# V rows of a PEER layer summed on TensorE as two column tiles of 64, with new places for the work of the next block

## The reference, cut to what matters

```python
def peer_ffn(h, w_q, keys, u, v):
    ...
    experts = ...                      # (token, 8 heads, 16): 128 expert numbers a token, of 16384
    g = jax.nn.softmax(best_s, axis=-1)
    def block(args):                   # 128 tokens at a time
        xt, et, gt = args
        act = jax.nn.gelu(jnp.einsum('td,thkd->thk', xt, u[et]), approximate=False)
        return jnp.einsum('thk,thkd->td', gt * act, v[et])
```

## Time and profile before

| | before |
|---|---|
| device time, median of 3 | 3504.54 us |
| device time of the profiled execution | 3502.22 us |
| its span, first to last instruction | 3500.1 us |
| granted TensorE clock, mean | 0.940 |
| bytes moved by DMA | 1346.12 MB, mean 385 GB/s |

### The profile page before, as it was taken

The page is one execution under the profiler, slowest core; times in us unless marked ns, Lnnn a source line. Parts: engine busy times, 40 slices in busy tenths (PEclk is TensorE's granted clock), DMA queues, the critical chain, the costliest instruction groups (busy, mean ns, idle before and its releaser), DMA issues.

```text
span 3500.1 us, 34723 instructions
## 1 busy us (share of the span) xinstructions
PE 2942.9 (84%) x10960; PEld 1660.0 (47%) x10960; DVE 2341.0 (67%) x5884; ACT 814.6 (23%) x1924; POOL 2008.2 (57%) x2085
## 2 busy tenths in 40 slices
PE   7786898888997899888987799888998789976777
PEld 6465355533554355444554445544554445522222
DVE  6229756886578765887477855786648866596554
ACT  3111421133111422133211332114221232211111
POOL 1003765666565664666555655666547655577775
PEclk9897999999999999999999999999999999998999
DMA  7787999999999999999999999999999999999998
GB/s 275 259 299 266 409 409 409 408 409 402 409 402 408 399 405 403 407 409 390 405 409 408 397 351 409 409 408 370 354 409 409 409 346 350 390 404 410 409 409 339
DMA packets 387256, 1346.12 MB, mean 385 GB/s; under 512 B 41793, under 2 KB 44865, under 8 KB 386433
## 3 DMA queue, kind: packets, MB, share of 16 engines
q0 software_dynamic: 294912, 1073.87, 78.0%
q1 hardware_dynamic: 91008, 265.83, 20.1%
q10 hardware_dynamic: 1152, 4.19, 0.3%
HBM read 1334.03 MB, written 35.39 MB: 391 GB/s over the span
## 4 chain that ended last, share of the span: by engine, by line
PE 43%; DMA 25%; DVE 14%; POOL 9%; issue 6%; ACT 3%; SPq 0%; DVEq 0%; ACTq 0%; POOLq 0%
PE ps_sum L1212 19%; DMA rows<-in_peer_u,ids_u 9%; PE ps_p L979 7%; DMA rows<-in_peer_v,ids_v 6%; DMA rows<-in_peer_v,ids_u 5%; POOL rows L802 5%; PE ps_s L1127 5%; POOL rows L792 4%; DVE rows L1986 4%; DMA w_ring<-packed 2%; PE ps_s L1065 2%; PE ps_p L1073 2%; DVE feat_b L1873 1%; PE ps_p L1047 1%; DVE feat_b L1869 1%
## 5 line engine op out<-in xcount | busy, mean ns | idle before, releaser
L1212 PE MATMUL ps_sum<-rows,diag 128*128 128x512 f32 x3584 | 1748.0, 631 | 271.9 <-DMA rows<-in_peer_v,ids_v 129.2
L1986 DVE CUSTOM_DVE_ANT_0 rows<-h_cur,rows 128x1024 f32<-128x1024 f32 x1024 | 1228.1, 1220 | 539.7 <-DMA rows<-in_peer_u,ids_u 527.0
L792 POOL DMA_INDIRECT rows<-in_peer_u,ids_u x1024 | 1005.4, 982 | 720.7 <-issue 498.8
L1212 PEld LDWEIGHTS ps_sum<-rows,diag 128*128 128x128 f32 x3584 | 684.1, 201 | 1166.4 <-issue 1047.8
L802 POOL DMA_INDIRECT rows<-in_peer_v,ids_v x512 | 493.5, 964 | 452.2 <-PE ps_sum L1212 295.6
L802 POOL DMA_INDIRECT rows<-in_peer_v,ids_u x512 | 494.4, 966 | 267.8 <-issue 127.3
L1466 ACT ACTIVATE diag<-ident,acts 128x128 f32<-128x128 f32 x896 | 327.4, 394 | 1057.4 <-PE ps_sum L1212 757.5
L979 PE MATMUL ps_p<-hT,w_ring 128*128 128x128 f32 x2944 | 367.8, 286 | 36.1 <-DMA w_ring<-packed 18.0
L979 PEld LDWEIGHTS ps_p<-hT,w_ring 128*128 128x128 f32 x2944 | 362.0, 202 | 68.6 <-issue 42.3
L1772 DVE CUSTOM_DVE_ANT_0 e<-ps_s,bias_t 128x256 f32<-128x256 f32 (+6 forms) x96 | 74.2, 773 | 177.5 <-PE ps_s L1065 70.6
L2007 DVE SCALAR_TENSOR_TENSOR x_cur<-rows,acts,x_cur 128x1024 f32<-128x1024 f32 x128 | 164.0, 1282 | 13.4 <-DMA rows<-in_peer_v,ids_v 13.4
(11 more groups left out here) (280 smaller groups left out, 2325.7 us busy)
## 6 DMA issues: line engine op xcount, KB each, us to landing
w_ring<-packed SPq DMA_DIRECT2D x343, 512.0 KB, 7.7
w_ring<-in_wstream SPq DMA_DIRECT2D x65, 512.0 KB, 5.3
packed<-in_wstream SPq DMA_DIRECT2D x49, 512.0 KB, 7.9
rows<-in_peer_u,ids_u POOLq DMA_INDIRECT x1024, 13.3
rows<-in_peer_v,ids_u POOLq DMA_INDIRECT x512, 10.7
rows<-in_peer_v,ids_v POOLq DMA_INDIRECT x512, 15.4
bias_rows<-rows SPq DMA_DIRECT2D x5, 1024.0 KB, 12.8
bias_t<-in_x SPq DMA_DIRECT2D x8, 512.0 KB, 6.2
```

The source lines that it names most:

```text
L792: pool.indirect_dma_start(u_rows[:, j % G_RING, :], None, peer_u, bass.IndirectOffsetOnAxis(ap=ids_u[:, j:j + 1], axis=0)).then_inc(u_land ...
L1212: ins = pe.matmul(ps_sum[:, c * 512:(c + 1) * 512], diag[:, n % 4, :], v_rows[:, j % G_RING, c * 512:(c + 1) * 512], start=(n == 0), stop= ...
L1986: dve.tensor_tensor_reduce(row, h_cur[:, :], row, 1.0, 0.0, ALU.mult, ALU.add, dots[:, p:p + 1]).then_inc(u_used, 1)
```

## The change

- V rows are summed in pairs. A gather of V no longer brings one row to each of 128 tokens, but two rows to each of 64: in an even gather partitions 0 to 63 and 64 to 127 hold two experts each of tokens 0 to 63, in an odd gather those of tokens 64 to 127. The diagonal matrix becomes 128x64, a 64x64 diagonal in its upper and in its lower half (`ident_pair` scaled by `coef`), so a product sums both halves. The even row goes to output partitions 0 to 63 (`low`), the odd row to 64 to 127 (`high`): two column tiles of TensorE. `add_rows` works on a pair at every odd position, with products in the order low, high, low, high, and waits for both rows' gathers and diagonals.
- All 128 rows go to TensorE; the eighth that VectorE took (`on_vector`, L2007, `v_added`) is gone.
- Expert numbers, gates and GELU results have to stand in the new order of partitions: `by_group` makes four copies of a quarter each where one stood (`hand_first_ids`, `hand_gates`, `hand_last_ids` on VectorE, the GELU on ScalarE). All V gathers now take `ids_v`.
- There are 8 diagonal buffers of 64 columns in place of 4 of 128. Some constants share memory with `acts` or `cols`.
- All three tables of stops have new numbers, other ones for each body.

The core of the diff; of the tables, which are long, the first body of TensorE's and VectorE's is shown in part:

```diff
 TENSOR_STOPS = [
...
-     "mla_2": (32, 33, 35), "mla_3": (35, 35, 37), "diff_0": (37, 38, 40, 41), "diff_1": (41, 43, 43, 44),
-     "diff_2": (45, 47, 48, 49), "diff_3": (49, 49, 51, 51), "join": (54, 56), "mix_out": (56, 56, 58, 58, 58),
-     "norm_cross": (59, 62), "cross_q": (62, 62, 62, 67, 67), "cross_scores": (69,), "cross_mix": (70, 73, 74),
...
+     "mla_2": (34, 34, 35), "mla_3": (35, 35, 35), "diff_0": (35, 43, 43, 43), "diff_1": (43, 43, 43, 50),
+     "diff_2": (50, 50, 50, 50), "diff_3": (50, 50, 55, 55), "join": (62, 62), "mix_out": (62, 62, 62, 62, 62),
+     "norm_cross": (62, 62), "cross_q": (62, 62, 62, 67, 67), "cross_scores": (67,), "cross_mix": (67, 73, 73),
...
 VECTOR_STOPS = [
...
-     "choose_0": (104, 105, 105, 105, 106, 108, 108, 108, 108, 111, 111), "top_1": (113, 113, 113, 113, 114, 117),
-     "choose_1": (120, 120, 124, 125, 126, 126, 126, 128, 128, 128, 128)},
...
+     "choose_0": (108, 108, 108, 108, 111, 111, 111, 111, 111, 111, 111), "top_1": (122, 122, 122, 122, 122, 122),
+     "choose_1": (122, 122, 122, 122, 122, 122, 122, 122, 122, 122, 122)},
...
-        diag = sb("diag", [P, 4, P])
+        diag = sb("diag", [P, DIAGS, GROUP])
+        ident_pair = sb("ident_pair", [P, GROUP])
...
+        def by_group(first, last):
+            for at, own in ((low, low), (low, high), (high, low), (high, high)):
+                column = slice(first + (own is high), last, 2)
+                row = slice(first + (at is high), last, 2)
+                yield at, column, own, row
...
-            def add_row(bp, p):
-                bp, j = row_of(bp, p, SUM_LAG)
-                if j is not None and not on_vector(j):
-                    n = sum_index(j)
-                    pe.wait_ge(diag_made, bp * SUM_ROWS + n + 1)
+            def add_rows(bp, p):
+                bp, last = row_of(bp, p, SUM_LAG)
+                if last is None or last % 2 == 0:
+                    return
+                pair = (last - 1, last)
+                pe.wait_ge(diag_made, bp * EXPERTS + last + 1)
+                for j in pair:
                     pe.wait_ge(v_landed[j % G_RING], bp * (16 * EXPERTS // G_RING) + 16 * (j // G_RING + 1))
...
-                    for c in range(2):
-                        ins = pe.matmul(ps_sum[:, c * 512:(c + 1) * 512], diag[:, n % 4, :], v_rows[:, j % G_RING, c * 512:(c + 1) * 512],
-                                        start=(n == 0), stop=(n == SUM_ROWS - 1), skip_group_check=True)
-                    ins.then_inc(v_used, 1)
+                for c in range(2):
+                    for j, own in zip(pair, (low, high)):
+                        ins = pe.matmul(ps_sum[own, c * 512:(c + 1) * 512], diag[:, j % DIAGS, :], v_rows[:, j % G_RING, c * 512:(c + 1) * 512],
+                                        start=(last == 1), stop=(last == EXPERTS - 1), skip_group_check=True)
+                        if c:
+                            ins.then_inc(v_used, 1)
...
-                    act.activation(acts[:, s * STEP:(s + 1) * STEP], dots[:, s * STEP:(s + 1) * STEP], ACT.Gelu).then_inc(acts_made, 1)
+                    for at, column, own, row in by_group(s * STEP, (s + 1) * STEP):
+                        ins = act.activation(acts[at, column], dots[own, row], ACT.Gelu)
+                    ins.then_inc(acts_made, 1)
...
-                    act.wait_ge(v_used, bp * SUM_ROWS + (n + SUM_SLOTS - 3))
-                    act.activation(diag[:, n % 4, :], ident[:, :], ACT.Copy, scale=coef[:, j:j + 1]).then_inc(diag_made, 1)
+                    act.wait_ge(v_used, bp * EXPERTS + (j + G_RING - DIAGS + 1))
+                    act.activation(diag[:, j % DIAGS, :], ident_pair[:, :], ACT.Copy, scale=coef[:, j:j + 1]).then_inc(diag_made, 1)
...
-                if j is not None and on_vector(j):
...
-                    dve.scalar_tensor_tensor(x_cur[:, :], v_rows[:, j % G_RING, :], coef[:, j:j + 1], x_cur[:, :], ALU.mult, ALU.add)\
-                       .then_inc(v_added, 1)
```

263 lines of the change are left out of this document (138 added, 125 removed), and 52 rows, old and new, of tables (SCALAR_STOPS, VECTOR_STOPS).

## The result

The changed kernel is slower: 3610.51 us at the median of five runs (3603.0 to 3631.6), beside 3504.54 us for the kernel before. The ratio is 1.0318, with a 95% interval of 1.0284 to 1.0351. The forecast was 3434 us.

The account below looks back on a forecast made before the run. Bound: DMA transfers at 409 GB/s, with TensorE limiting the dips. 3502.2 - 79 (dips) + 2 + 5 + 5 (what stays) + 1.5 (start) - 5.5 (end) = 3431.2; with 2.3 to the median, 3434 us; range 3415 to 3500.

Parts of the forecast that it names:

- The ceiling: From 350 us on, DMA transfers set the pace wherever the rate is 409 GB/s; a faster engine gives nothing there.
- TensorE is the limit there: In three short dips of the transfer rate (14.9, 19.6, 23.7 us), TensorE, 90 to 93% busy, sets the pace.
- rival 4: Dips stay because something other than TensorE, an attention chain, makes them: 3500 to 3505 us; chance 0.08 together with rival 3.
- The factor of 0.571: TensorE's V sums: both tiles of a pair overlap, so a block takes 111 us in place of 195.
- TensorE's busy time with 0.43 of L1212 taken away, against what the DMA needs: In the dips: 55.6, 68.5, 73.0 us against 65.1, 80.4, 76.3, so the DMA becomes the limit; 2 us stay.
- The turns: TensorE drains at tiling mode changes: 0.2 us each, two per group of pairs, 7 us a body against 84 saved.
- one position later: V ring: a pair's even buffer comes free only with the odd one, 2.56 us later; no cost was summed.
- rival 3: The ring of 8 V buffers becomes the bound and GpSimd stands there: about 3500 us; chance 0.08 together with rival 4.
- The stops: New stops make longer front end bursts; the DMA runs dry 4 us in the first body, 5 us in all.
- rival 2: Tiles overlap in part, or new stops leave gaps (28 us): either about 3460 us, both 3490; chance 0.12.
- The end: After the last gather, TensorE's V sums keep up with the DMA and finish 5.5 us earlier.
- rival 1: TensorE's two column tiles run one after the other: 3575 us, between 3540 and 3640; chance 0.14.

Follow-up runs that it names:

- the kernels with 64 and 72 columns: Kernel before with only the first of each V row's two products, made 64 or 72 columns wide in place of 128: 3525.0 us and 3495.1 us.

## Why the prediction was wrong

The ladder, in ratios to the kernel before times 3504.5 us; each step carries 6 to 16 us of uncertainty:

| step | from, to | us |
|---|---|---|
| TensorE's V work halved | 1, 0.9965 | -12 |
| its products 64 columns wide: turns | 0.9965, 1.0059 | +33 |
| the rest of the tiles: second products, VectorE's rows, copies, GELUs | 1.0059, 1.0087 | +10 |
| both rows of a pair waited for together | 1.0087, 1.0171 | +29 |
| the new stops | 1.0171, 1.0318 | +52 |

The steps join different kernels, and each says what its edit did in that place. The +33 of the turns was measured on a kernel with 298 of them each way and half of the products; the changed kernel has 158, and what they cost there was not measured.

**The ceiling** held: no slice of the changed kernel is above 409 GB/s, and it moves the same 1346 MB. It is not the same on every chip (361 GB/s on one of the slower ones).

**"TensorE is the limit there"** held in part. Its V products, which stand between the links of the attention, could be halved for 12 us; its value products, which are links themselves, counted for 20 to 31 of 34 us. So it is TensorE's work in the order of the chain that the dips wait for, more than its total load. Of rival 4, a chain of the attention, the part that names something other than TensorE has no support in ScalarE's link; the value products were halved on the slower chips only, and VectorE's links were not tried.

**The factor of 0.571** held: a pair costs 1.72 us, 1.74 were taken. L1210's busy time is 1225 us and not 900 to 1100; a part of it ran at half the clock (3.68 us a pair).

**The step that failed first** is "TensorE's busy time with 0.43 of L1212 taken away, against what the DMA needs". It subtracted work at a clock of 0.96 and kept that clock for the rest. The halved products show what comes in its place: 62 us of work away in the dips, 12 us of time gained, TensorE still 86 to 88% busy, at 0.76 to 0.85. That the lower clock takes most of the difference is read from the traces: the rest of TensorE's work in the attention of bodies 3 to 6 grew from 147 to 183 us of busy time while L1212's fell from 158 to 109, and two executions of the same instructions differ by 8 us in one body at clocks of 0.74 and 0.84. By the estimate above some 30 us of the dips hang on the clock. The 16 to 20 us that would stay at full clock are a second error of the same step: it let the transfers run at 409 GB/s as soon as TensorE's busy time was below theirs, although the heads' chain leaves TensorE idle between links (43 of 348 us in these stretches before, 64 of 356 with half of the products). No run changes the clock and nothing else, and the one that raised it did so by work of its own. The prediction named this for the last block's retrieval ("the clock can take some of it back"), found it covered there by the transfers, and didn't ask it of the dips, where the transfers don't cover it.

**The turns** were priced and then not summed. The estimate of 0.2 us a drain was right in size (0.20 and 0.14 measured). The section "Key Properties" of the Trainium skill's "TensorEngine Tiling (Array Packing)", by which a change of the tiling mode drains TensorE, is borne out by the kernels with 64 and 72 columns. The count was right too: the changed kernel has 18 groups of V products in its first body, as many as the table has stops, and 158 in all, 54 us of TensorE's time, 8 us a body where 7 were taken. What kept them out is that they were set against the 84 us saved in a body as a whole, as if any time that TensorE saves could pay for them. With the old stops they are more (298 in the kernel before), and there 33 of 101 us reached the end. The sentence that the front end stays in the full mode is wrong in part: it has products of 128x64 and of 64x128 and 32x128, in the kernel before too; what their turns cost was not looked at.

**Pairs and rings**: "one position later" was costed at nothing. It cost 29 us (21 by medians). GpSimd's waits for TensorE grew above 419.5 us while TensorE was less busy, which the prediction had named as the sign of rival 3. Its price for a slower landing did not apply: 8.2 us is the page's median now, where it was 15.4 for one half of the V gathers and 10.7 for the other; what counted was the wait for both rows, fewer and longer than row by row (up to 6.9 us against 2.9).

**The stops** were the largest error in a single term: 5 us were taken, 52 measured. The prediction looked for bursts on VectorE in the choice of experts, and took a burst of front end work to be harmless as long as it is shorter than the ring (rival 2 put them at 28 us at most). The place at 729 to 745 us shows what it missed: TensorE waits with V products queued behind the waiting instruction, and then runs a bundle, at a lower clock. With the old stops V rows lie in that place. That is one place of many; which places make up the 52 us was not counted.

**Covered, as predicted:** the four GELUs (0 us). ScalarE's waits for TensorE at the diagonals fell from 757 to 227 us, as it had said, and diagonals of half the width last 338 ns where 394 was the bound. The three handover copies weren't run by themselves; they are within the +10, which is hardly told from zero.

**The end** came 2 us earlier relative to the last gather, not 5.5: the last V sum ends 8.3 us after the last gather's issue (3612.7 to 3621.0), where it was 10.5.

```profile
3612.71 0.94 POOL L797 DMA_INDIRECT rows<-in_peer_v,ids_v  x1 [0.30 <-issue]
...
3619.05 1.94 PE L1210 MATMUL ps_sum<-rows,diag 128*64 128x512 f32 x8 [0.58 <-DMA rows<-in_peer_v,ids_v]
```

**The range and the chances.** The range ended at 3500 because everything that could go wrong, rival 1 aside, was made a share of a gain of 79 us. Three of the terms that went wrong (turns, joined rows, stops) are costs that exist without any gain, and each had a sentence in the forecast that put it at nothing or at 5 us. Measured they are 33 (on the kernel with half of the products), 29 and 52 us; the only rival of the slower side, rival 1, held none of them. Its range of 3540 to 3640 takes in the measured time, but by luck: its tiles one after the other did not come.

**Still open:** how much of the 29 us is the longer wait and how much the lower clock that comes with less work; why single positions of the stops in the kernel before are worth 21 us; and what the clock alone takes in the dips, beyond the estimate above. Of the faster kernels in this study all leave part of the work out; none that computes everything beats the kernel before.

## What to carry to other kernels

Where a granted clock follows the load, work taken from the busiest engine is not time: cost the gain again at the clock that the lighter engine would be granted, and ask whether the work taken away is a link of the chain that the dip waits for or stands between its links. Count the turns between forms of products (full array, column tiles) by the groups of the kernel as it will be, and put them into the sum where nothing covers them. When two waits are joined, or pieces of work bundled, price the longest stretch in which the ring's consumer stands still, the wait ahead of the bundle included.

## What was not expected of the hardware

- Two 64 wide column tiles overlap completely in f32: a pair costs 1.72 us in a closed run, as one 128 wide row does, in either order of the products.
- A turn into the 64 wide form costs 0.20 us, one out of it 0.14 us; 72 columns cost neither.
- With half of the V products the mean granted clock fell from 0.94 to 0.80, and in the dips from 0.96 or 0.97 to between 0.76 and 0.85. It was not the same in two executions of that kernel: 0.74 and 0.84 in the same stretch.
- The kernel before took 3502 to 3505 us on three chips and 3711 to 3715 us on three others. There few slices reach 409 GB/s; why was not studied.
